# The second FFN's input matmuls as two-by-two block products with seven products in place of eight

## What is computed

```python
D_MODEL, SEQ, D_FF = 1024, 512, 2816

def swiglu(u, w_in, w_out):
    a, b = jnp.split(u @ w_in, 2, axis=-1)
    return (jax.nn.silu(a) * b) @ w_out
...
        u = modulate(rms_norm(h, g_ffn2[l]), sh3, sc3)
        h = h + 0.5 * gt3 * swiglu(u, w_ffn2_in[l], w_ffn2_out[l])
```

## Time and profile before

| | |
|---|---|
| time, median of 3 runs (range) | 1333.25 us (1332.83 to 1337.33) |
| the profiled execution's own time | 1337.59 us |
| its span in the profile | 1335.7 us |
| PE busy | 1259.3 us, 94% of the span |
| DVE busy | 672.4 us, 50% |
| ACT busy | 616.6 us, 46% |
| POOL busy | 70.0 us, 5% |
| second FFN's input, pairs 2 to 21 | 987.4 to 1205.0 us of the span |

### The profile page before, as it was taken

The page is one execution under the profiler, slowest core; times in us unless marked ns, Lnnn a source line. Parts: engine busy times, 40 slices in busy tenths (PEclk is TensorE's granted clock), DMA queues, the critical chain, the costliest instruction groups (busy, mean ns, idle before and its releaser), DMA issues.

```text
span 1335.7 us, 17907 instructions
## 1 busy us (share of the span) xinstructions
PE 1259.3 (94%) x6505; PEld 1015.1 (76%) x6505; DVE 672.4 (50%) x953; ACT 616.6 (46%) x1121; POOL 70.0 (5%) x102
## 2 busy tenths in 40 slices
PE   2699999999999799999988999999799999999998
PEld 2588888887777577777857878787578888888887
DVE  6766666565443563664457356564533333332221
ACT  5476666665443454555575333543332223221221
POOL 3000000000111000000121111001100000000000
PEclk8699999999999899999989999999899999999999
DMA  9467666777662222222212111463223333343320
GB/s 326 118 170 184 182 183 180 185 206 201 160 156 63 63 80 79 63 64 79 80 50 62 49 49 49 128 189 95 63 79 97 102 99 94 94 118 108 103 83 29
DMA packets 279955, 152.36 MB, mean 114 GB/s; under 512 B 7877, under 2 KB 275294, under 8 KB 279902
## 3 DMA queue, kind: packets, MB, share of 16 engines
q1 hardware_dynamic: 275678, 149.54, 40.4%
q10 hardware_dynamic: 4224, 2.10, 0.5%
HBM read 145.31 MB, written 6.29 MB: 113 GB/s over the span
## 4 chain that ended last, share of the span: by engine, by line
PE 88%; DVE 4%; ACT 3%; SPq 2%; issue 1%; DMA 0%; ACTq 0%; DVEq 0%
PE tail L1313 13%; PE region L1313 13%; PE region L1314 13%; PE region L1315 13%; PE tail L1315 13%; PE tail L1314 13%; PE region L1469 2%; SPq L382 1%; PE region L1331 1%; PE region L1455 1%; PE region L1504 1%; PE region L1342 1%; PE region L1533 1%; ACT w_hi L525 1%; PE region L1621 1%
## 5 line engine op out<-in xcount | busy, mean ns | idle before, releaser
L525 ACT ACTIVATE w_hi<-raw 128x1024 fp32r<-128x1024 f32 (+1 forms) x181 | 201.7, 1115 | 532.3 <-PE tail L1315 276.9
L879 DVE TENSOR_TENSOR w_lo<-raw,w_hi 128x1024 fp32r<-128x1024 f32 (+1 forms) x181 | 234.4, 1295 | 288.0 <-ACT w_hi L525 286.3
L1313 PE MATMUL region<-u_hi,w_hi 128*128 128x512 f32 x672 | 266.2, 396 | 3.7 <-DVE w_lo L879 3.7
L1314 PE MATMUL region<-u_lo,w_hi 128*128 128x512 f32 x672 | 262.3, 390 | 0.0
L1315 PE MATMUL region<-u_hi,w_lo 128*128 128x512 f32 x672 | 262.3, 390 | 0.0
L1313 PEld LDWEIGHTS region<-u_hi,w_hi 128*128 128x128 f32 x672 | 126.6, 188 | 33.1 <-issue 4.7
L1314 PEld LDWEIGHTS region<-u_lo,w_hi 128*128 128x128 f32 x672 | 126.4, 188 | 28.5 <-issue 2.4
L1313 PE MATMUL tail<-u_hi,w_hi 128*128 128x512 f32 x344 | 144.7, 421 | 1.9 <-DVE w_lo L879 1.9
L1315 PEld LDWEIGHTS region<-u_hi,w_lo 128*128 128x128 f32 x672 | 126.6, 188 | 26.3
L1313 PE MATMUL tail<-g_hi,w_hi 128*128 128x512 f32 x352 | 141.1, 401 | 0.0
L1314 PE MATMUL tail<-g_lo,w_hi 128*128 128x512 f32 x352 | 139.0, 395 | 0.0
(11 more groups left out here) (286 smaller groups left out, 1492.7 us busy)
## 6 DMA issues: line engine op xcount, KB each, us to landing
raw<-in_w_ffn_in SPq DMA_DIRECT2D x176, 256.0 KB, 3.4
ada_raw<-in_w_ada SPq DMA_DIRECT2D x56, 512.0 KB, 5.0
raw<-in_w_in SPq DMA_DIRECT2D x90, 256.0 KB, 3.3
raw<-in_w_ffn_out SPq DMA_DIRECT2D x32, 384.0 KB, 5.1
raw<-in_w_ffn_out SPq DMA_DIRECT2D x32, 320.0 KB, 3.6
ada_early<-in_w_ada SPq DMA_DIRECT2D x8, 1024.0 KB, 11.9
gates<-kept_gates SPq DMA_DIRECT2D x16, 256.0 KB, 4.0
raw<-in_w_out SPq DMA_DIRECT2D x16, 256.0 KB, 3.2
```

The source lines that it names most:

```text
L525: act.activation(w_hi[:, slot % 2, 0:k, :], raw[:, slot, 0:k, :], ACT.Copy).then_inc(hi_ready, 1)
L879: dve.tensor_tensor(w_lo[:, slot % 2, 0:k, :], raw[:, slot, 0:k, :], w_hi[:, slot % 2, 0:k, :].bitcast(f32), ALU.subtract).then_inc(lo_rea ...
L1313: pe.matmul(bank(b), wh, xh, start=start and n == 0, stop=False)
L1314: pe.matmul(bank(b), wh, xl, start=False, stop=False)
```

## The change

A two-by-two block product needs eight block products done plainly and seven done in Winograd's form, at the price of sums on both sides. The change does this for pairs 2 to 21 of the second FFN's input. A pair's two units are the two columns of weight blocks, the 1024 inputs are cut into two halves of 4 chunks, and the 512 positions into two halves of 256 columns (`TH`). Pairs 0 and 1 (`PLAIN`) stay as they were.

- **PE**: `product` issues one block product: 4 chunks x 3 matmuls of 256 columns. Seven of them make a pair, P1 to P7 below in program order; each increments `p_ps`.
- **Input sums**, once: `mixed_u` holds four sums and differences of quarters of `u`, made by five DVE and three POOL instructions of 1024 elements per partition, and split by ACT into `tt_hi` (and one quarter of `u_hi`) and by DVE into `tt_lo`.
- **Weight sums**, for every pair: four POOL instructions of 512 elements (`weight_sums`, s1 to s4), two into `sums_raw` (in the memory of `ssq` and `rstd`) and two in place in `raw`.
- **Splits**: in place of two per pair there are four groups: g0 (the loaded blocks), g1 (`sums_raw`), g2 (the sums in place), each 1024 elements, and g3, 512 elements. `ring_hi` and `ring_lo` make them.
- **Joins**: a block product is needed in several results. ACT copies three banks to `prods` (`p_copy`), DVE adds them to other banks (three instructions of 256 elements), and the final multiply with Silu's result is two of 256 elements.
- **Loads**: the same transfers. Slot b of a pair is now also held until POOL's third sum.
- `ada_acc` moves into memory that overlaps the FFN's own buffers, and the program asks for a smaller scratch area for dynamic DMAs; no instruction follows from either.

The core of the diff:

```diff
+            def ring_hi(i, jj, g):
+                m = seven(i, jj)
+                a, b = f2_slot(2 * jj), f2_slot(2 * jj + 1)
+                if g == 0:
+                    act.wait_ge(raw_in[a], f2_loads(i, 2 * jj))
+                    source = raw[:, a, 0:8, :]
+                elif g == 1:
+                    act.wait_ge(sums_ready, 4 * m + 2)
+                    source = sums_raw
+                elif g == 2:
+                    act.wait_ge(sums_ready, 4 * m + 4)
+                    source = raw[:, a, 0:8, :]
+                else:
+                    source = raw[:, b, 4:8, :]
...
+                act.activation(ring(w_hi, jj, g), source, ACT.Copy).then_inc(hi_ready, 1)
...
+            for i in laps(act, KF // 2, 2):
...
+                for jj in range(2):
+                    m, j, last = seven(i, jj), 2 * i + jj, is_static(i) and i > 1 and jj == 1
+                    x, y = bank(3 * jj), bank(3 * jj + 1)
+                    p_copy(m, 0, 1, x)
+                    ring_hi(i, jj, 2)
+                    ring_hi(i, jj, 3)
+                    p_copy(m, 2, 3, x)
+                    p_copy(m, 1, 4, y)
+                    split_hi(F2_OUT, 0, 0) if last else ring_hi(i + jj, 1 - jj, 0)
+                    act.wait_ge(p_joined, 3 * m + 3)
+                    if not last:
+                        ring_hi(i + jj, 1 - jj, 1)
+                    silu(j, work[:, 0, :])
+                    if last:
+                        split_hi(F2_OUT, 0, 1)
+                    gated_hi(j)
```

POOL's sums for one pair:

```diff
+                pool.tensor_tensor(sums_raw[:, 0:4, :], b[:, 0:4, :], b[:, 4:8, :], ALU.add).then_inc(sums_ready, 1)
...
+                pool.tensor_tensor(sums_raw[:, 4:8, :], sums_raw[:, 0:4, :], a[:, 0:4, :], ALU.subtract)\
+                    .then_inc(sums_ready, 1)
+                pool.wait_ge(lo_ready, group(i, jj, 0) + 1)
+                pool.tensor_tensor(a[:, 0:4, :], a[:, 0:4, :], b[:, 0:4, :], ALU.subtract).then_inc(sums_ready, 1)
+                pool.wait_ge(sums_ready, 4 * m + 2)
+                pool.tensor_tensor(a[:, 4:8, :], a[:, 4:8, :], sums_raw[:, 4:8, :], ALU.subtract).then_inc(sums_ready, 1)
```

PE's seven products, of which the third adds to the bank that the first has filled and ACT has copied:

```diff
+                    pe.wait_ge(lo_ready, group(i, jj, 0) + 1)
+                    product(x, jj, 0, 0, *u_part(0, half_1), True)
+                    product(z, jj, 0, 4, *u_part(4, half_1), True)
+                    pe.wait_ge(lo_ready, group(i, jj, 1) + 1)
+                    pe.wait_ge(p_copied, 3 * m + 1)
...
+                    product(x, jj, 1, 4, *t_part(0), False)
...
+                    product(y, jj, 1, 0, *u_part(0, half_2), True)
+                    pe.wait_ge(lo_ready, group(i, jj, 2) + 1)
+                    pe.wait_ge(p_copied, 3 * m + 2)
+                    product(x, jj, 2, 0, *t_part(1), False)
+                    pe.wait_ge(p_copied, 3 * m + 3)
+                    product(y, jj, 2, 4, *u_part(4, half_2), False)
+                    pe.wait_ge(lo_ready, group(i, jj, 3) + 1)
+                    pe.wait_ge(p_joined, 3 * m + 2)
+                    product(x, jj, 3, 0, *t_part(2), False)
```

More of the change, by code:

```diff
@@ L141, in build @@
         raw = sb("raw", [P, RAW, HALF, P])
[L142 removed]
+        w_hi, w_lo = sb("w_hi", [P, 2, HALF + 1, P], f32r), sb("w_lo", [P, 2, HALF + 1, P], f32r)
         ident, ones = sb("ident", [P, P]), sb("ones", [P, P])
@@ new lines, in _, with p_copy @@
+            act.wait_ge(glu_ready, KF + 1)
+            silu(1, bank(3))
+            ring_hi(1, 0, 1)
+            t_high(3, u_hi[:, 0:4, half_2], 1)
+            gated_hi(1)
+            def p_copy(m, n, ps, b):
+                act.wait_ge(p_ps, 7 * m + ps)
+                if not (is_static(m) and m == 0):
+                    act.wait_ge(p_joined, 3 * m - 3 + n + 1)
+                act.activation(prods[:, (0, 2, 1)[n], :], b[:, half_1], ACT.Copy).then_inc(p_copied, 1)
+            for i in laps(act, KF // 2, 2):
+                if is_static(i) and i == 0:
+                    continue
+                for jj in range(2):
+                    m, j, last = seven(i, jj), 2 * i + jj, is_static(i) and i > 1 and jj == 1
[13 more added lines that the diff above has]
+                    gated_hi(j)
@@ new lines, in _ @@
+            t_low(3, u_lo[:, 0:4, half_2], u_hi[:, 0:4, half_2], 1)
+            gated_lo(1)
+            for i in laps(dve, KF // 2, 2):
+                if is_static(i) and i == 0:
+                    continue
+                for jj in range(2):
+                    m, j, last = seven(i, jj), 2 * i + jj, is_static(i) and i > 1 and jj == 1
+                    x, y, z = (bank(3 * jj + n) for n in range(3))
+                    dve.wait_ge(p_ps, 7 * m + 2)
+                    dve.wait_ge(p_copied, 3 * m + 1)
+                    dve.tensor_tensor(work[:, 0, half_1], prods[:, 0, :], z[:, half_1], ALU.add).then_inc(p_joined, 1)
+                    ring_lo(i, jj, 2)
+                    ring_lo(i, jj, 3)
+                    dve.wait_ge(p_ps, 7 * m + 5)
+                    dve.wait_ge(p_copied, 3 * m + 3)
+                    dve.tensor_tensor(work[:, 1, half_2], prods[:, 2, :], x[:, half_1], ALU.add).then_inc(p_joined, 1)
+                    split_lo(F2_OUT, 0, 0) if last else ring_lo(i + jj, 1 - jj, 0)
+                    dve.wait_ge(p_ps, 7 * m + 6)
+                    dve.tensor_tensor(work[:, 0, half_2], prods[:, 1, :], y[:, half_1], ALU.add).then_inc(p_joined, 1)
+                    if not last:
+                        ring_lo(i + jj, 1 - jj, 1)
+                    dve.wait_ge(silu_ready, KF + j + 1)
+                    dve.tensor_tensor(work[:, 1, half_2], work[:, 0, half_2], work[:, 1, half_2], ALU.mult)
+                    dve.wait_ge(p_ps, 7 * m + 7)
+                    dve.tensor_tensor(work[:, 1, half_1], work[:, 0, half_1], x[:, half_1], ALU.mult).then_inc(glu_ready, 1)
+                    if last:
+                        split_lo(F2_OUT, 0, 1)
+                    gated_lo(j)
@@ L1706, in _, with product @@
             statistics(2)
-            ffn_in(1, F2_IN)
+            def product(dst, jj, g, w0, x_hi, x_lo, start, wait=None):
+                for k in range(4):
+                    wh, wl = ring(w_hi, jj, g)[:, w0 + k, :], ring(w_lo, jj, g)[:, w0 + k, :]
+                    xh, xl = x_hi[:, k, :], x_lo[:, k, :]
+                    pe.matmul(dst[:, half_1], wh, xh, start=start and k == 0, stop=False, skip_group_check=not start)
+                    pe.matmul(dst[:, half_1], wh, xl, start=False, stop=False, skip_group_check=not start)
+                    ins = pe.matmul(dst[:, half_1], wl, xh, start=False, stop=k == 3, skip_group_check=not start)
+                ins.then_inc(p_ps, 1)
```

172 lines of the change are left out of this document (158 added, 14 removed).

## The result

The changed kernel takes 1368.58 us, median of 4 runs (1365.73 to 1370.88), where the kernel before takes 1333.16 (1332.83 to 1337.33) beside it: 35.4 us more, a ratio of 1.0257 with a 95% interval of 1.0225 to 1.029. It is slower, as forecast, by 35.4 us where 27.8 were forecast; 1361 was 7.6 us too low, and inside the range. The profiled execution took 1370.88, with a span of 1369.2 against 1335.7: 33.5 more.

A forecast was written before the change was run, and what follows sets the result against it. It took PE, by matmul count and spacing, to bound the kernel before. Waits of 9.0 + 4.8 + 18 x 1.75 = 45.3 us against 17.7 saved gave 27.6 slower: 1333.25 + 27.6 = 1361 us, range 1342 to 1378.

The forecast's parts named there:

- 1.5 to 2 that were named: Sign of being right: in every pair PE idles 1.5 to 2 us ahead of the third product, released by ACT's copy.
- the chain: Hand-overs between DVE and ACT from the fifth product's end to the next pair's third: 7.45 us, making the period 11.75.
- the block: POOL and DVE exclude each other, the later standing still; POOL's fourth sum delays the `w_lo` of g1 by 0.8 us.
- (b): Rival: POOL's third and fourth sums fall where DVE joins or idles, so they miss the chain; 1347 us, chance 0.12.
- (e): Rival, no change: POOL does not block DVE, signals and register instructions cost half; period 10.6, 1335 us, chance 0.07.
- (f): Rival: weights, not columns, pace PE, 0.17 us per 256-column matmul, 14.3 us a pair; 1401 us, chance 0.04.
- The saving: PE's matmuls over 20 pairs: a pair falls from 10.88 to 10.0 us, 17.7 us saved if nothing waits.
- The waits of 18 pairs: PE stands 1.75 us ahead of the third product in each of 18 pairs.
- a wait at that place: Sign of being wrong: PE's idle time lies ahead of the fifth product, for POOL's fourth sum.
- The start: First block pairs: the third product starts 9.0 us late, and late POOL makes the first period 4.8 us longer.
- If DVE asks first, the multiply waits at the same price: If DVE precedes POOL's fourth sum, its multiply with two SBUF inputs waits for that sum instead, also 0.8 us.
- (d): Rival, faster: hand-overs leave the chain, which falls below 5.7 us, so only the start costs; 1325 us, chance 0.07.
- (c): Rival: the clock falls at many of the 1.75 us waits; 1371 us for one pair in three, 1391 for each; chance 0.10.

The follow-up runs named there:

- e2: The changed kernel with POOL's four weight sums cut to 8 elements each, so its products are not the right ones: 1339.73 us.
- e11: The changed kernel with one more wait: POOL's second sum of a pair waits for the `w_lo` of the last pair's g3: 1361.29 us.
- e6: The changed kernel with the next pair's first copy, join and g2, g3 splits ahead of `g_hi` and `g_lo`, and POOL's weight sums cut to 8 elements: 1324.76 us.
- e3: The changed kernel with POOL's fourth sum also waiting for the `w_lo` of the next pair's g1: 1361.61 us.
- e7: The changed kernel with the next pair's first copy, join and g2, g3 splits ahead of `g_hi` and `g_lo`, POOL's second sum behind g3's `w_lo`: 1328.99 us.
- e1: The changed kernel with ACT's copy of the next pair's first product moved ahead of this pair's `g_hi`: 1368.78 us.
- e8: e7 with the early start of e4: 1325.19 us.
- e4: The changed kernel with three DVE sums and two differences of `u` moved earlier, and POOL's first sum released sooner: 1362.85 us.
- e12: e9 with the seventh product's sum of `u` moved behind the first pair's first four products: 1322.55 us.
- e9: e7 with another start: DVE also does POOL's three instructions on `u`, and POOL's first weight sum waits for the first `w_lo` of g0: 1322.87 us.

## Why the prediction was right, and where its sizes were off

The mechanism was right: PE idles 1.47 us a pair ahead of the third product (just under the 1.5 to 2 that were named), released by ACT's copy; the chain behind it took 7.33 us for 7.45; the `w_lo` from the sums has a mean of 2.09 us; the first product comes 5.5 us late; the clock is 1.00 behind the start. Of the period's two causes e2 and e11 give the sizes: with the block in the chain alone it is 11.61 (e11; forecast 11.75), without any block 10.76 (forecast 10.95). So the block costs the chain 0.85 us, where 0.80 was taken. The signals and register instructions, for which no row stood in the trace of before, took 0.19 us from the third join to the split of g1 (0.24 taken) and 0.14 from the second multiply to `g_hi` (0.16 taken). Rival (b), that the block misses the chain, is refuted by that, (e), which needed no block, by the stretched `w_lo`, and (f) by the 9.84 of e6.

The sum, term by term, in the profiled execution:

- **The saving.** Forecast 17.7, measured 20.8: matmuls are 0.117 apart, not 0.119.
- **The waits of 18 pairs.** Forecast 18 x 1.75 = 31.5. Measured: from the second pair's third product (1016.16) to the last pair's (1231.15) are 18 periods, 215.0 us, where 9.84 each would be 177.1: 37.9, some 2.1 a pair. The mis-sized step is the chain's: it followed the block to the `w_lo` from the sums and took `g_lo` at its own 0.68. `g_lo` asks for the port 0.02 us behind the second sum, takes 1.80, and everything behind it on DVE is late up to the `w_lo` of g2. That makes a second wait, ahead of the fifth product: 12.05 - 11.61 = 0.44 us a pair. The prediction had named a wait at that place, for another sum, as a sign that it was wrong; a fifth of what a pair loses is there (0.44 of 12.05 - 9.84 = 2.21 us).
- **The start.** Forecast 9.0 + 4.8 = 13.8; measured 9.9 for the third product (1000.14 for 990.2) and 16.02 - 9.84 = 6.2 for the first period, 16.1. Of that, 0.7 us is no work of the change: the second FFN's input began later by it, in code that had not changed (959.52, and 958.85 before). The fifth product waits 2.24 us, and behind it the clock is at 0.50 from 1006.5 to 1009.9; 16 matmuls at 0.213 for 0.117 are 1.5 us of the 2.3 that the term is short.
- Together 16.1 + 37.9 - 20.8 = 33.2 us, where 13.8 + 31.5 - 17.7 = 27.6 were forecast; the spans differ by 33.5. That the medians differ by 35.4 and not by 33.5 is within the spread of single runs. The waits and the start were 8.7 us too low and the saving 3.1, and these errors cancel in part: that 1361 lies so near is some luck.

Two statements behind the sum fell. "If DVE asks first, the multiply waits at the same price": in e3 the period stayed, but the price went to the `w_lo` of g2, two instructions on. And rival (d), that only with no block could the hand-overs leave the chain and make it faster: in e7 the `w_lo` from the sums is blocked as long as before (2.10) and the profile shows no wait of PE. What decided was not the length of the block but what stood behind it, in the order of ACT and DVE. Where (d) was said to need 0.95 us less of closely priced instructions, an order that takes `g_hi` and the copy out of the chain gives that much. Rival (c), the clock, was left out of the middle by the changed kernel, but is real: e1 shows it once.

## What to carry to other kernels

A product saved on PE is worth its columns only if the hand-over chain of a tile is shorter than the products that can run meanwhile; write that chain down from signal to signal, and put each engine's instructions that PE waits for ahead of those that only finish the last tile. Here two reorderings and one wait (e7) turned 35 us of loss into 5 us of gain with the same instructions, and a start that was made before it was needed gave 3.8 us more (e8). Two engines that exclude each other can share a tile, if each long instruction of the one is released by a signal at which the other has slack; a sum that starts as soon as its data are there is not the cheapest sum.

## What the runs showed of the hardware that was not expected

- The length of a wait alone does not say whether the clock falls. In e1 PE stood still for 1.86 us ahead of a product at 1037.45 (1.42 a pair before); 1.4 us later matmuls are 0.2 apart, and the granted clock of the stretch is 0.77:

```profile
1037.45 0.38 PE L1963 MATMUL region<-tt_hi,w_hi 128*128 128x256 f32 x1 [1.86 <-DVE w_lo L1499]
...
1036.00:1041.00 5.00, 3.55 (x21) 3.56 (x22) 3.46 (x5) 1.03 (x2) 0.00 (x0) 0.77 0.42 123
```

  That period of e1 is some 1.5 us longer than the mean of 11.88. The 1.47 us waits of the changed kernel did not do it from 1010 on (1.00), nor did a later wait of 1.86 us in e1 itself, at 1073.68, nor one of 3.14 us at the start of e4 (992.93):

```profile
1073.00:1080.00 7.00, 6.32 (x54) 6.33 (x55) 4.43 (x6) 2.19 (x4) 2.55 (x2) 1.00 0.53 150
...
993.00:1010.00 17.00, 12.82 (x103) 12.24 (x104) 14.05 (x14) 7.51 (x12) 10.29 (x7) 1.00 0.22 64
```

  The first row is of e1, the second of e4. Behind the 3.15 us wait of e12 (996.84) the granted clock was 0.51 from 997.0 to 1000.5. What decides between them is open here.
- The block needs no measurable lead: 0.02 us decided which of DVE and POOL had the port, and cost DVE 1.15 us. The page "SBUF — State Buffer" of the Trainium skill, section "Who interferes with whom", says that the one that issues first has it for the whole instruction. The runs agree, but for the end: the blocked one ends 0.55 us (`g_lo`, 0.68 long) and 1.08 us (`w_lo`, 1.22 long) behind the other, so some 0.14 us of its own time lie beside the end of the first. DVE instructions with an input in PSUM were not stretched beside POOL in any run (0.40 to 0.42 us for 256 elements).
- POOL needs 2.4 us of the port for what DVE does in 1.14 (1024 elements in each partition): the second of the three on u took 2.38 us in the changed kernel, at 986.65, and the first 2.44 in e8, at 974.53. Giving all three to DVE (e9) brought the third product 1.1 to 1.5 us forward and no gain in time clear of the spread, since it still waited for POOL's weight sums and ACT's split.
